# Attention units of a two-layer transformer block on one core: fillers of the input projection divided over two places, compression products moved ahead of a unit's scores, two products nobody reads added

## The reference, cut to what matters

```python
for layer in range(2):
    h = rmsnorm(x, norm_mix[layer])
    z = h @ w_in[layer]                      # 1024 x 2964, split into 19 parts
    o_a = nsa_mixer(...)     # softmax over compressed, selected and windowed keys
    o_b = diff_mixer(...)    # difference of two softmaxes
    o_c = mlstm_mixer(...)   # gated linear attention
    o_d = dilated_mixer(...) # softmax with counted, dilated keys
    x = x + concat([o_a, o_b, o_c, o_d]) @ w_out[layer]
    h = rmsnorm(x, norm_ffn[layer])
    x = x + (silu(h @ w_gate[layer]) * (h @ w_up[layer])) @ w_down[layer]
```

## Time and profile before

| what | value |
| --- | --- |
| median of 3 runs | 2054.19 us (2051.68 to 2054.51) |
| the profiled execution's own time | 2057.17 us |
| its span, first to last instruction | 2055.3 us |
| TensorE busy with products | 1890.7 us, 92% of the span |
| VectorE, ScalarE, GpSimd busy | 42%, 16%, 4% |
| mean granted TensorE clock | 0.973 of full speed |
| the 14 units, layer 0 | 76.7 us to about 180 us of the span |
| the 14 units, layer 1 | 477.1 us to about 580 us of the span |

### The profile page before, as it was taken

How to read it: one execution, slowest core, us unless ns; L and a number is a source line. 1 busy time by engine, 2 the same in 40 slices (tenths; PEclk the granted TensorE clock), 3 DMA queues, 4 the chain that set the end, 5 groups by cost and what they waited for, 6 DMA issues and landing times.

```text
span 2055.3 us, 21126 instructions
## 1 busy us (share of the span) xinstructions
PE 1890.7 (92%) x8030; PEld 962.3 (47%) x8030; DVE 863.4 (42%) x1560; ACT 332.1 (16%) x783; POOL 86.6 (4%) x129
## 2 busy tenths in 40 slices
PE   8988999999899998999999999997998988988885
PEld 4555664455556644855434333333875333323221
DVE  1466987834768877854111111113325111111113
ACT  2442111133421102121101000001002000000000
POOL 4102000001020002100000000000000000000000
PEclk9999999999999999999999999999999999999998
DMA  9214886751168877465999999999254999999995
GB/s 309 86 57 142 303 292 244 254 184 42 57 209 295 294 267 243 148 233 209 365 427 428 428 427 428 428 426 403 106 202 178 423 428 428 428 428 427 427 426 211
DMA packets 149242, 603.14 MB, mean 293 GB/s; under 512 B 16584, under 2 KB 60536, under 8 KB 121232
## 3 DMA queue, kind: packets, MB, share of 16 engines
q1 hardware_dynamic: 144064, 591.43, 73.0%
q0 software_dynamic: 4880, 10.22, 1.9%
q10 hardware_dynamic: 192, 0.05, 0.0%
HBM read 597.67 MB, written 1.10 MB: 291 GB/s over the span
## 4 chain that ended last, share of the span: by engine, by line
PE 62%; DMA 22%; DVE 8%; DVEq 2%; issue 2%; ACT 2%; ACTq 1%; SPq 1%
PE ps L2491 15%; DMA ring<-in_e_w_gate 14%; PE ps L910 12%; DMA ring<-in_e_w_up 7%; PE ps L638 7%; PE ps L2323 4%; PE ps L2509 4%; PE ps L2255 3%; PE ps L2336 3%; PE ps L993 3%; PE ps L734 2%; PE ps L2435 2%; PE ps L2420 1%; DMA ring<-in_e_w_down 1%; PE ps L718 1%
## 5 line engine op out<-in xcount | busy, mean ns | idle before, releaser
L2491 PE MATMUL ps<-ring,hT 128*64 128x512 f32 (+1 forms) x1056 | 242.5, 611 | 34.0 <-DMA ring<-in_e_w_gate 19.9
L2509 PE MATMUL ps<-ring,qkT 128*64 128x512 f32 (+1 forms) x1024 | 226.6, 594 | 10.5 <-ACT qkT L2711 8.0
L2491 PE MATMUL ps<-ring,late 128*32 128x512 f32 (+1 forms) x928 | 207.9, 601 | 24.7 <-DMA ring<-in_e_w_up 12.8
L638 PE MATMUL ps<-ring,hT 128*128 128x512 f32 (+1 forms) x384 | 171.1, 597 | 2.8 <-DMA ring<-in_w_in 2.0
L2491 PEld LDWEIGHTS ps<-ring,hT 128*64 128x64 f32 (+1 forms) x1056 | 77.0, 126 | 195.9 <-issue 195.9
L2980 DVE TENSOR_TENSOR qkT<-ps,qkT 128x512 f32<-128x512 f32 (+1 forms) x64 | 44.2, 690 | 256.2 <-PE ps L2509 256.2
L3003 DVE TENSOR_TENSOR qkT<-ps,qkT 128x512 f32<-128x512 f32 (+1 forms) x32 | 22.1, 690 | 296.4 <-PE ps L2491 296.4
L2491 PEld LDWEIGHTS ps<-ring,late 128*32 128x32 f32 (+1 forms) x928 | 67.8, 124 | 160.1 <-issue 160.1
L2509 PEld LDWEIGHTS ps<-ring,qkT 128*64 128x64 f32 (+1 forms) x1024 | 70.8, 123 | 146.9 <-issue 146.9
L1616 DVE SCALAR_TENSOR_TENSOR qkT<-ring,cc,qkT 128x512 f32<-128x512 f32 x168 | 125.9, 749 | 8.6 <-issue 0.4
L638 PEld LDWEIGHTS ps<-ring,hT 128*128 128x128 f32 x384 | 73.4, 198 | 80.7 <-issue 71.0
(11 more groups left out here) (433 smaller groups left out, 2226.8 us busy)
## 6 DMA issues: line engine op xcount, KB each, us to landing
ring<-in_e_w_down SPq DMA_DIRECT2D x64, 2048.0 KB, 17.3
ring<-in_e_w_up SPq DMA_DIRECT2D x64, 2048.0 KB, 17.3
ring<-in_e_w_gate SPq DMA_DIRECT2D x60, 2048.0 KB, 17.2
ring<-in_ada_w SPq DMA_DIRECT2D x24, 2048.0 KB, 14.0
ring<-in_w_gate SPq DMA_DIRECT2D x16, 1408.0 KB, 7.8
ring<-in_w_up SPq DMA_DIRECT2D x16, 1408.0 KB, 8.7
ring<-in_w_down SPq DMA_DIRECT2D x22, 1024.0 KB, 5.0
ring<-in_w_in SPq DMA_DIRECT2D x8, 2048.0 KB, 11.6
```

The lines of the kernel that those rows point to most:

```text
L638: last = mm(m.ps[:, 4 + i, 0:chunk_width(n)], m.hT[:, j, i * P:(i + 1) * P], w[:, j, :], start=(j == 0), stop=(j == KC - 1))
L2491: last = mm(dst, xg[:, j, at + x * n_tok:at + x * n_tok + place], w(x, j), start=(j == 0), stop=(j == KC - 1))
L2509: lasts[x] = mm(dst, m.hidT[:, j, rows + x * place:rows + (x + 1) * place], half_of(w(x, j), n), start=(j == 0), stop=(j == 3))
```

## The change

Three kinds of edit, all on TensorE; no other engine's program is changed.

1. `z_terms` computes any run of a chunk's eight products (`z_part` now calls it). Each filler of four products, u below 8, is divided: two products ahead of `transposed(u)`, two ahead of `values(u)`. Likewise half of the output projection's part that stood ahead of the values of unit 11 (its second column half) now stands ahead of the transposes of unit 12.
2. `cmp_batch` stands ahead of `scores(4)` instead of behind it.
3. Two products of 512 columns that nothing reads, into bank 3, stand ahead of `scores(10)`.

```diff
-        def z_part(n, i, part):
+        def z_terms(n, i, terms):
...
-            for j in range(KC // 2 * part, KC // 2 * (part + 1)):
+            for j in terms:
                 last = mm(m.ps[:, 4 + i, 0:chunk_width(n)], m.hT[:, j, i * P:(i + 1) * P], w[:, j, :], start=(j == 0), stop=(j == KC - 1))
-            if part == 1:
+            if terms[-1] == KC - 1:
                 last.then_inc(s["z_ps"], 1)
+
+        def z_part(n, i, part):
+            z_terms(n, i, range(KC // 2 * part, KC // 2 * (part + 1)))
...
-        def out_part(i, first):
+        def out_part(i, first, columns=(0, 1)):
 
-            for c in range(2):
+            for c in columns:
...
+        def z_quarter(u, second):
+
+            first = KC // 2 * (u % 2) + KC // 4 * second
+            z_terms(C_VALUES if u < 4 else C_DIL, u // 2 % 2, range(first, first + KC // 4))
+
+        def ahead_of_transposes(u):
+
+            if u < 8:
+                z_quarter(u, 0)
+            elif u == 12:
+                out_part(0, 2, (1,))
+
         def ahead_of_values(u):
 
-            if u < 4:
-                z_part(C_VALUES, u // 2, u % 2)
-            elif u < 8:
-                z_part(C_DIL, u // 2 - 2, u % 2)
+            if u < 8:
+                z_quarter(u, 1)
...
             elif u == 11:
                 out_ready(1)
-                out_part(0, 2)
+                out_part(0, 2, (0,))
...
+        def unread(count):
+
+            for _ in range(count):
+                mm(m.ps[:, 3, :], m.ident[:], bcast(m.ones[:].unsqueeze(1), [P, 4, P]), start=True, stop=True)
+
+        def ahead_of_scores(u):
+
+            if u == 2:
+                cmp_batch()
+            elif u == 8:
+                unread(2)
+
         def behind_scores(u):
 
             if u == 1:
                 diff_batch()
-            elif u == 2:
-                cmp_batch()
...
         for u in range(N_UNITS):
+            ahead_of_transposes(u)
             transposed(u)
             ahead_of_values(u)
             values(u)
+            ahead_of_scores(u)
             if u + 2 < N_UNITS:
                 scores(u + 2)
             behind_scores(u)
```

More of the change, by code:

```diff
@@ L627, in first_tensor @@
         pe.wait_ge(s["hT_s"], nth(L, "hT_s", 4))
-        def z_part(n, i, part):
+        def z_terms(n, i, terms):
             c = CHUNKS[n][0]
-            if part == 0:
+            if terms[0] == 0:
                 if i == 0:
```

## The result

The changed kernel took 2040.92 us (median of 4 runs, 2039.96 to 2043.22), the kernel before 2053.65 us beside it (4 runs). The ratio is 0.9938, 95% interval 0.9925 to 0.9952. The forecast was 2047.9 us with a range down to 2042.5 us: the sign and the mechanism were right, and the gain forecast (6.3 us) was half of the measured one.

A forecast was written before the change was run, and what follows sets the result against it. TensorE's waits and the lower clock behind them bound the 14 units. A layer gains 7.2 - 3.4 = 3.8 us, both 7.6, less 1.3 is 6.3: 2047.9 us; own range 2045 to 2051, 8 in 10 runs 2042.5 to 2055.

The forecast's parts named there:

- The walk without spells: TensorE's order in layer 0 stepped forward with durations kept: 7.2 us gained a layer, 6.9 clock and 0.3 waits and order.
- The price of a spell: A stretch of TensorE at the lower granted clock (0.50, 1.2 GHz) costs about 1.7 us; layer 0 had four, 6.9 us.
- Spells that stay: Low-clock stretches left in the 14 units after the change: two a layer, 2 x 1.7 = 3.4 us.
- I count one here ... I count one for both: One low-clock stretch at 95.1 to 100.3 us, one shared by the waits ahead of scores(3) and around scores(13).
- The stretch from 95 to 100 us: Unit 2's values to the quarter behind scores(4): no large product, 1.7 us of waits, compression; one low-clock stretch counted.
- The new wait ahead of scores(3): Behind unit 1's transposes, 4.5 us cover a 6.2 us chain: 1.7 us wait, sharing one counted low-clock stretch with scores(13).
- that of scores(13): scores(13), moved ahead, wait 1.3 us for unit 12's exponentials; one low-clock stretch counted jointly with the wait at scores(3).
- I take 1.3 us of these 3.0 as spells in these units that the median doesn't have: Profiled execution was 3.0 us above the median; 1.3 us of that taken off the 7.6 us gain, leaving 6.3 us.
- the clean case: Rival: all low-clock stretches in both layers' units go, 2 x 7.2 = 14.4 us, 2042.8 us from the profiled execution; chance 0.14.
- the moved case: The rival "The spells only move" as the range's upper side, about 2053.6 us; chance 0.26.
- The spells only move: Rival: new waits ahead of scores(3), (4), (13) get low-clock stretches, four a layer again; 0.3 us a layer left; chance 0.26.
- slower: Rival: quarters ahead of ready transposes delay the chain to the scores, units 3 to 9 too; 5 us slower, 2059 us; chance 0.08.

The follow-up runs named there:

- division only: Kernel before with only the z fillers of units 0 to 7 divided; compression behind scores(4), no unread products, unit 12's part undivided: 2057.77 us, ratio 1.0016.

## Why the prediction was right about the mechanism and wrong about the size

- **What bounds the units: right.** Almost all the gain is clock. Unread products in five places, with nothing divided or moved, give 12.5 us, as much as the change.
- **The walk without spells: right.** It gave 7.2 us a layer, of it 6.9 us of clock; the other term, 0.3 us, doesn't come out of the figures beside it (11.7 less 10.0 less 1.8 is -0.1 us). The one layer of the changed kernel without a spell is 6.5 us shorter. Counted from the small transposes, scores(4) are 0.75 us late in layer 0 (24.21 for 23.46 us; 0.8 forecast), with the compression already done. Unit 5's transposes in layer 1 start at 39.80 us against 39.82 before in layer 0 (level was forecast). The transposes of unit 12 in layer 1 start at 84.97 us against 90.54 before in layer 0 (5.6 us earlier was forecast). scores(10) have no wait. The idle time went from 12.6 to 10.1 us in layer 1, and from 12.9 to 9.5 us in layer 0.
- **The price of a spell: right where nothing waits behind it.** 1.7 us, by the pair with and without the unread products. By the lengths of two layers it is 1.7 us in the changed kernel (112.16 for 110.50 us), and 0.5 us in the one divided in units 0, 5 and 7 (106.47 for 105.96 us).
- **The step that failed: "Spells that stay", and in it two terms.** First, "I count one here ... I count one for both", two spells a layer. The two profiles of the changed kernel have 2 and 0, 2 and 1: 1.25 a layer. The stretch from 95 to 100 us, which I took as the surest place, had none of them; its 1.6 us of waits are in two pieces with the compression between. The new wait ahead of scores(3), one of the two that I gave one spell between them, had two of the five, and that of scores(13) two more; the fifth, at 106.09, stood where none was forecast and where no wait is near. Second, "I take 1.3 us of these 3.0 as spells in these units that the median doesn't have". Two more profiles of the kernel before show the units as long as in the first, so nothing was to be taken off. Units alone: 234.8 us before (117.76 + 117.03), 223.6 and 225.2 us after, 10.4 us on average where the forecast ended at 6.3. The two terms make up this difference: 1.5 spells fewer at 1.7 us are 2.6 us, and with the 1.3 us that is 3.9 of the 4.1 us.
- **The bound of the range.** It was the clean case counted from the profiled execution, 2042.8 us, while the moved case was counted from the median. Since the profiled execution's surplus was not in the units, the clean case from the median is 2054.2 - 14.4 = 2039.8 us. The measured 2040.92 us lies between the two.
- **What no term had: about 2 us behind the units.** From the last mark to the end of the span, the three profiles of the kernel before have 1462.5, 1458.4 and 1460.9 us, the two of the changed kernel 1458.8 and 1457.8 us. The stages there are not touched and vary with their own spells. Of the other kernels, all but one lie between 1457.0 and 1458.9 us; division only has 1460.9 us. The windows over this part, in the first profile of the kernel before and in that of the changed one:

```profile
592.77:2055.30 1462.53, 1338.36 (x5848) 644.16 (x5848) 493.77 (x822) 161.77 (x334) 29.33 (x36) 0.97 0.84 341
```

```profile
579.45:2038.20 1458.75, 1333.56 (x5848) 642.45 (x5848) 493.52 (x822) 161.66 (x334) 29.36 (x36) 0.98 0.85 342
```

For the same 5848 instructions TensorE is busy 1338.4, 1333.5 and 1337.5 us in the profiles of the kernel before, 1333.6 and 1333.0 us in those of the changed one. The record of the granted clock has it at the lower level for 83.3, 75.3 and 78.3 us against 71.6 and 67.9 us. So this gap of 2.3 us on average goes with the clock too. Why the lower level is rarer there, by chance or by when the experts' stages begin, is open.
- **The rivals.** "Clean" was nearest by its number, but that is luck: only one layer in four was clean. "The spells only move" is refuted for the whole change but is close to what division alone does, and there the "slower" rival's mechanism shows too: 1.0016. The kernel divided only at units 0, 5 and 7 shows the rival's price inside the change: 4 us a layer, hidden in the change by what the clock gave.
- **The rule cited from the Trainium skill** ("TensorE: Matmul & The Clock Gate", section "Why this matters for your kernels") would have made filling these waits worth 0.6 us, as the prediction worked out. The runs disagree: 12.5 us from unread products put where TensorE waited 0.99 to 2.20 us.

## What to carry to other kernels

Where transposes and other small products stand around a wait of 1 or 2 us, look at the products behind it: if they are sometimes longer, the stretch costs the wait and the lower clock too. Large products put there, even unread ones, paid for themselves in this kernel, also at unit 0, where they start its transposes 0.8 us later and save 1.7 us. They don't always help (one of ten places kept its spell), and small products without any wait can have a spell too. Divide a filler only where a wait stands ahead; moved ahead of work that is ready, it delays whatever chain that work starts on the other engines. Walk the order forward for the waits, but take the number of spells from several profiles, since their places change between executions of one kernel.

## What was not expected of the hardware

The same wait is followed by the lower clock in one execution and not in the next: behind the 0.99 us ahead of unit 0's transposes the eight products took 5.30 us in the first profile of the kernel before and 3.60 us in the second.

The lower clock also came without a wait: in the changed kernel at 106.09, after 8.09 us in which TensorE never stood idle and whose last 3.5 us held small products only. In another execution and in layer 1 the same products at the same place had none. What it shares with the spells behind waits is the small products ahead of it; whether a wait adds to it was not tried by itself.

And a spell doesn't always cost 1.7 us: the second profile of the kernel before counts five in layer 0 where the first has four, and both are 117.75 us long. Part of it can be read: the wait of 1.02 us ahead of unit 5's transposes isn't there in the second profile, whose two spells just ahead of it took its place. The rest lies at unit 12, where the double stretch costs 2.9 us for 1.7 (transposes and products 1.97 and 5.65 us, for 1.63 and 4.79 us in the earlier trace rows, and 1.09 and 3.60 us at the full clock). Against these stand the spells at unit 0 and behind scores(10), which the second profile doesn't have.
